# The up projection of a ConvFFN in seven block products, and its down projection after a detour through device memory

## The chip, the cores and the metric

The kernel runs on one core of one Trainium2 chip, as one program. The metric is the device time of one execution in microseconds. Three runs of the kernel before took 1481.65, 1480.47 and 1481.75 us (median 1481.65).

The engines are named as the profile names them: PE (TensorE, matrix products; PEld its weight loads), DVE (VectorE), ACT (ScalarE), POOL (GpSimd) and SP (the queue that issues most DMAs).

## What is computed

One layer of a streaming encoder works on 1024 prompt rows and 64 sample rows of 1024 channels, in fp32. After an input projection, two convolution mixers and a merge, the ConvFFN follows, and a final norm:

```python
h = rms_norm(x, norm2_g)
f_gate, f_val = jnp.split(h @ w_up, 2, axis=-1)           # w_up: 1024 x 5632
f_gate, new_f = causal_dwconv(f_gate, st_f, dw_f)          # 3 taps along time
x = x + (jax.nn.silu(f_gate) * f_val) @ w_down             # w_down: 2816 x 1024
```

Outputs are the normed rows of both groups and the last rows that each convolution saw.

## The kernel before

Activations lie with channels on the 128 partitions and time along the free dimension, W = 1092 columns (two rows of history, 1024 prompt rows, two of history, 64 sample rows). 1024 channels are KD = 8 tiles, the 2816 channels of the ConvFFN are KF = 22 feature tiles. An fp32 product is made from three reduced ones: each operand is split into a high half (rounded to the matmul's type) and a low half (the rest), and `products` (line 396) issues weight-high x activation-high, weight-high x activation-low, and weight-low x activation-high into one PSUM accumulation.

A "unit" (line 424) is one tile of 128 output channels over all columns: three thirds of 364 columns (362 in the first), for each third 8 k tiles of 3 matmuls, 72 matmuls in all. Units use the three PSUM banks of X and the three of Y in turn; S is a third, smaller area. For each unit SP loads 512 KB of weights (`load`, line 275), ACT makes the high half (`split_hi`, line 699), DVE the low half (`split_lo`, line 959), both two units ahead; semaphores count each step.

The ConvFFN stage starts at unit N_F. A loop over eleven groups (`ffn_units`, line 635) takes two feature tiles per turn: gate unit, value unit, gate unit, value unit, and between the first and the second the down projection of the group before (`down`, line 622): 8 output tiles x 3 thirds x 2 k tiles x 3 matmuls, added to the residual by DVE (`add_down`, line 1267). The residual `stream` and the running squares of the rows are kept on chip. The first gate unit starts third by third as the last unit of w_o is added up (lines 885 and 1214 to 1222). The reciprocal root of the mean square is not applied to h but to the products: column sums of squares on PE (`rms_columns`, line 601), `moments` on DVE (line 1132), a power on POOL (line 384), a diagonal matrix on DVE (line 1136), a row broadcast by PE (`rms_row`), and copies by ACT into rb2 (lines 913 and 914).

Per feature tile DVE multiplies the gate by rb2, puts in the two history columns, saves the last two, and applies three taps (lines 1229 to 1247); ACT takes silu (line 901); DVE multiplies by rb2 and by the value unit (lines 1251 and 1256); ACT and DVE split the result in halves (lines 905 and 957), which are the k tiles of the down projection. The last group is done in cuts of 386, 384 and 322 columns (lines 1324 to 1351), together with the transposes and the final norm of the output rows.

The order of the work on each engine is written out by hand; nothing is planned by a compiler.

Of the kernel before, what the change touches and what calls it, by code (L numbers as in the profile page):

```python
# [14 lines left out]
def streaming_encoder(nc: bass.Bass, ins, outs):  # L15
# [46 lines left out]
    G = KF // 2  # L62
# [6 lines left out]
    X_F1, Y_F1 = X_F0 + 2, Y_F0 + 2  # L69
    X_DL = X_F1 + 6 * (G - 1)  # L70
# [12 lines left out]
    Q_F = KB + 2 * KA  # L83
# [35 lines left out]
    q_hi, _ = place("q_hi", [P, KA, W], F32R)  # L119
# [3 lines left out]
    w_raw, _ = place("w_raw", [P, 2, KD * P], F32)  # L123
    w_hi, _ = place("w_hi", [P, 2, KD * P], F32R)
    w_lo, _ = place("w_lo", [P, 2, KD * P], F32R)
    t0, _ = place("t0", [P, W], F32)
    t1, _ = place("t1", [P, W], F32)
    xr, _ = place("xr", [P, 3 * D], F32)
# [4 lines left out]
    state_rows, _ = place("state_rows", [P, 4, P], F32)  # L133
# [7 lines left out]
    wd_raw = mid[:, 0:2 * D]  # L141
    wd_hi, _ = place("wd_hi", [P, 2, D], F32R, mid_at + 4 * 2 * D)
    wd_lo, _ = place("wd_lo", [P, 2, D], F32R, mid_at + 4 * 4 * D)
    rb2 = mid[:, 6 * D:6 * D + W]
    gf_row = mid[:, 6 * D + SW:7 * D + SW]
    assert 7 * D + SW <= KD * W
    out_rows, _ = place("out_rows", [P, NT, D], F32, h_at)
# [15 lines left out]
    sl, ac = xr[:, 0:W], xr[:, W:2 * W]  # L163
# [3 lines left out]
    half = stats[:, 5 * NT:6 * NT]  # L167
    ST_B = 2 * HA * KA
# [10 lines left out]
    with ExitStack() as ctx:  # L179
        X = ctx.enter_context(nc.psum_tensor("X", [P, CHUNKS, 512], F32))  # L180
        Y = ctx.enter_context(nc.psum_tensor("Y", [P, CHUNKS, 512], F32))
# [34 lines left out]
        value_part, ac_part, qhi_part, qlo_part = sem("value_part"), sem("ac_part"), sem("qhi_part"), sem("qlo_part")  # L216
        last_added = sem("last_added")

# [19 lines left out]
        F_STEPS = 6  # L238
# [28 lines left out]
        def _(sp):  # L267
# [51 lines left out]
            with sp.Fori(0, G) as i:  # L319
                load(w_up_cols, 2 * P * i, N_F, 4, i)  # L320
                load(w_up_cols, DF + 2 * P * i, N_F + 1, 4, i)
                load(w_up_cols, 2 * P * i + P, N_F + 2, 4, i)
                load(w_up_cols, DF + 2 * P * i + P, N_F + 3, 4, i)
                sp.wait_ge(hlo_done, KD)

                sp.dma_start(wd_raw.rearrange("p (k c) -> p k c", k=2),
                             w_down_rows[bass.ds(i, 1), :, :, :].rearrange("g p k c -> p (g k) c")
                             ).then_inc(wd_in, 16)
            sp.dma_start(gf_row, ins["final_g"].rearrange("(a d) -> a d", a=1).to_broadcast([P, D])).then_inc(gf_in, 16)

            n_out = 0
            sp.wait_ge(s_out, S_STATE + 1)
            for s, group in enumerate(("p", "s")):
                sp.dma_start(outs[f"new_conv_a_{group}"].rearrange("l b r (c p) -> (l b r c) p", p=P),
                             state_rows[0:HA * KA, s, :]).then_inc(stored, 16)
                sp.dma_start(outs[f"new_conv_b_{group}"].rearrange("l b r (c p) -> (l b r c) p", p=P),
                             state_rows[s * H * KB:(s + 1) * H * KB, 2, :]).then_inc(stored, 16)
            sp.wait_ge(s_out, S_FST + 1)
            for s, group in enumerate(("p", "s")):
                sp.dma_start(outs[f"new_ffn_conv_{group}"].rearrange("l b r (c p) -> (l b r c) p", p=P),  # L340
                             state_rows[s * H * KF:(s + 1) * H * KF, 3, :]).then_inc(stored, 16)
# [53 lines left out]
        def _(pe):  # L395
# [191 lines left out]
            unit(N_WO + 1, 2, i, y_out, Y_WO + i, KD, h_hi, h_lo, part=wo_part)  # L587

# [8 lines left out]

            def ffn_in(c):
                return lambda k: pe.wait_ge(hlo_done, KD + KD * c + k + 1)
# [6 lines left out]
            def rms_row(part):  # L606
                def run():
                    if part == 0:
                        pe.wait_ge(stat_step, KD + 2)
                    pe.wait_ge(s_out, S_R2 + part)  # L610
                    row_of(diag, part)()
                return run

            unit(N_F, 0, 0, x_out, X_F0, KD, h_hi, h_lo, (None, None, rms_columns), before=ffn_in)
            unit(N_F + 1, 0, 0, y_out, Y_F0, KD, h_hi, h_lo, (rms_row(0), rms_row(1)))
            unit(N_F + 2, 0, 0, x_out, X_F0 + 1, KD, h_hi, h_lo)
            unit(N_F + 3, 0, 0, y_out, Y_F0 + 1, KD, h_hi, h_lo)
# [3 lines left out]

            def down(group, x_use, y_use):

                pe.wait_ge(wdlo_done, group + 1)
                pe.wait_ge(qlo_done, KB + 2 * KA + 2 * group + 2)
                for m in range(KD):
                    b, free, uses = ((Y, y_out, y_use), (X, x_out, x_use))[m % 2]
                    pe.wait_ge(free, uses + m // 2)
                    for c in range(CHUNKS):
                        for k in range(2):  # L630
# [751 lines left out]
```

## Time and profile before

| | us |
|---|---|
| median of three runs | 1481.65 |
| span of the profiled execution, first to last instruction | 1479.4 |
| PE busy / PEld busy | 1456.1 / 1448.6 |
| DVE busy / ACT busy / POOL busy | 781.2 / 308.7 / 26.4 |
| ConvFFN: its first matmul starts | 665.41 |
| last group's tail: its first matmul starts | 1436.69 |

The profiled execution's own time is not listed apart from its span; the runs lie 1.1 to 2.4 us above the span. Busy time counts an engine's recorded instructions; overlapping ones count once. The end of a matmul is modelled, so recorded durations (330 ns for 364 columns) are longer than the step from one start to the next. "Idle before" is the time that an engine had nothing running ahead of an instruction, and the arrow names what ended it.

### The profile page before, as it was taken

To read this page: it belongs to the slowest core of one execution; us is meant where nothing else is said; L and a number is where in the kernel's file an instruction comes from. 1 tells how busy PE (TensorE), PEld (TensorE's weight loads), DVE (VectorE), ACT (ScalarE), POOL (GpSimd) and SP (SyncE) were. 2 spreads that over 40 slices of the span, in tenths; PEclk is the share of its full clock that TensorE was granted. 3 is DMA by queue.
4 is the path that set the end of the run, shared out by engine and by line. 5 is a ranking of instruction groups with operands and counts; after the bars stand their busy time and mean duration, and the time that the engine had idled before them with its cause. 6 is when DMAs were issued, how large, how long until landed. Compare 5 with 4: busy or idle time off the path is not lost.

```text
span 1479.4 us, 20930 instructions
## 1 busy us (share of the span) xinstructions
PE 1456.1 (98%) x8774; PEld 1448.6 (98%) x8774; DVE 781.2 (53%) x744; ACT 308.7 (21%) x329; POOL 26.4 (2%) x57
## 2 busy tenths in 40 slices
PE   6999999999999999999999999999999999999997
PEld 6999999999999999999999999999999999999997
DVE  5575888755642225346635363545454535354545
ACT  5321111111252214134111111111111111101012
POOL 3000000000000000000000000000000000000001
PEclk9999999999999999999999999999999999999999
DMA  5111111111022222112202020201010101010103
GB/s 188 53 43 43 43 43 43 41 45 43 29 72 71 71 71 64 43 43 72 72 15 71 14 71 14 71 26 59 28 57 28 57 28 57 28 57 29 61 2 121
DMA packets 107898, 77.18 MB, mean 52 GB/s; under 512 B 2469, under 2 KB 101527, under 8 KB 107863
## 3 DMA queue, kind: packets, MB, share of 16 engines
q1 hardware_dynamic: 106631, 72.22, 15.6%
q10 hardware_dynamic: 1232, 4.46, 0.9%
q8 instruction: 26, 0.43, 0.1%
q14 instruction: 9, 0.07, 0.0%
HBM read 72.04 MB, written 4.63 MB: 52 GB/s over the span
## 4 chain that ended last, share of the span: by engine, by line
PE 98%; DVE 1%; DMA 0%; POOL 0%; ACT 0%; issue 0%; DVEq 0%; SPq 0%
PE X L400 48%; PE Y L400 47%; PE S L562 1%; DMA xr<-in_x_prompt 0%; PE S L510 0%; PE Y L455 0%; DVE out_rows L1336 0%; PE S L668 0%; PE S L528 0%; PE Y L668 0%; POOL stats L377 0%; PE S L455 0%; DVE h_lo L957 0%; ACT h_hi L717 0%; DVE res L1345 0%
## 5 line engine op out<-in xcount | busy, mean ns | idle before, releaser
L400 PE MATMUL X<-h_hi,w_hi 128*128 128x364 f32 (+1 forms) x1056 | 347.7, 329 | 2.6 <-issue 2.4
L400 PE MATMUL X<-h_lo,w_hi 128*128 128x364 f32 (+1 forms) x1056 | 348.3, 330 | 0.0
L400 PE MATMUL Y<-h_lo,w_hi 128*128 128x364 f32 (+3 forms) x1056 | 347.6, 329 | 0.0
L400 PE MATMUL Y<-h_hi,w_hi 128*128 128x364 f32 (+3 forms) x1056 | 347.3, 329 | 0.0
L400 PE MATMUL X<-h_hi,w_lo 128*128 128x364 f32 (+1 forms) x1056 | 346.9, 329 | 0.0
L400 PE MATMUL Y<-h_hi,w_lo 128*128 128x364 f32 (+3 forms) x1056 | 346.3, 328 | 0.0
L957 DVE TENSOR_TENSOR w_lo<-w_raw,w_hi 128x1024 fp32r<-128x1024 f32 (+1 forms) x104 | 118.7, 1142 | 415.5 <-ACT w_hi L704 415.5
L704 ACT ACTIVATE w_hi<-w_raw 128x1024 fp32r<-128x1024 f32 (+1 forms) x104 | 103.2, 993 | 798.7 <-PE Y L400 485.9
L400 PEld LDWEIGHTS X<-h_hi,w_hi 128*128 128x128 f32 x1056 | 199.1, 189 | 3.4 <-issue 2.8
L400 PEld LDWEIGHTS Y<-h_hi,w_hi 128*128 128x128 f32 x1056 | 198.5, 188 | 0.6 <-issue 0.5
L400 PEld LDWEIGHTS X<-h_hi,w_lo 128*128 128x128 f32 x1056 | 199.0, 188 | 0.0
L400 PEld LDWEIGHTS X<-h_lo,w_hi 128*128 128x128 f32 x1056 | 199.0, 188 | 0.0
L400 PEld LDWEIGHTS Y<-h_lo,w_hi 128*128 128x128 f32 x1056 | 198.4, 188 | 0.5 <-issue 0.5
L400 PEld LDWEIGHTS Y<-h_hi,w_lo 128*128 128x128 f32 x1056 | 198.4, 188 | 0.0
L1010 DVE SCALAR_TENSOR_TENSOR res<-mid,cols,res 128x1118 f32<-128x1118 f32 (+1 forms) x120 | 165.7, 1381 | 18.0 <-DVE res L1010 17.8
L400 PE MATMUL X<-q_hi,wd_hi 128*128 128x364 f32 (+4 forms) x276 | 91.1, 330 | 0.0
L400 PE MATMUL X<-q_lo,wd_hi 128*128 128x364 f32 (+4 forms) x276 | 91.0, 330 | 0.0
L400 PE MATMUL X<-q_hi,wd_lo 128*128 128x364 f32 (+4 forms) x276 | 90.6, 328 | 0.0
L400 PE MATMUL Y<-q_lo,wd_hi 128*128 128x364 f32 (+4 forms) x252 | 83.1, 330 | 0.0
L400 PE MATMUL Y<-q_hi,wd_hi 128*128 128x364 f32 (+4 forms) x252 | 83.0, 329 | 0.0
L400 PE MATMUL Y<-q_hi,wd_lo 128*128 128x364 f32 (+4 forms) x252 | 82.7, 328 | 0.0
L1272 DVE TENSOR_TENSOR res<-X,res 128x1092 f32<-128x1092 f32 x40 | 51.8, 1294 | 39.4 <-PE X L400 39.3
(166 smaller groups left out, 1380.4 us busy)
## 6 DMA issues: line engine op xcount, KB each, us to landing
w_raw<-in_w_up SPq DMA_DIRECT2D x44, 512.0 KB, 3.7
w_raw<-in_w_in SPq DMA_DIRECT2D x36, 512.0 KB, 3.7
mid<-in_w_down SPq DMA_DIRECT2D x11, 1024.0 KB, 5.9
xr<-in_x_prompt SPq DMA_DIRECT2D x8, 512.0 KB, 3.8
xr<-in_x_prompt ACTq DMA_DIRECT2D x8, 512.0 KB, 4.3
w_raw<-in_w_o SPq DMA_DIRECT2D x8, 512.0 KB, 3.4
out_y_prompt<-out_rows SPq DMA_DIRECT2D x8, 512.0 KB
w_raw<-in_w_b_out SPq DMA_DIRECT2D x8, 256.0 KB, 2.6
```

The source lines that it names most:

```text
L400: done = pe.matmul(dst, w, act[:, k, cols[0]:cols[1]], start=(first and p == 0), stop=(last and p == 2))
L562: last = pe.transpose(S[:, k // 4, (k % 4) * P:(k % 4) * P + rows], xr[0:rows, s * D + k * P:s * D + (k + 1) * P], ident[0:rows, 0:rows])
L704: act.activation(w_hi[:, s, 0:k_tiles * P], w_raw[:, s, 0:k_tiles * P], ACT.Copy).then_inc(whi_done, 1)
L957: dve.tensor_tensor(out, full, hi.bitcast(F32), ALU.subtract).then_inc(done, 1)
L1010: dve.scalar_tensor_tensor(dst, mid[:, bass.ds(U_AT + c * UW + k, CVW)], col("dw_a", k * KA + c), dst, ALU.mult, ALU.add).then_inc(tap_don ...
L1272: dve.tensor_tensor(x, bank(bk), x, ALU.add).then_inc(out, 1)
```

## The change

**w_up in seven block products.** For one feature tile f, the gate tile and the value tile are computed together. The 8 k tiles are halved into even and odd ones, the 1092 columns into two halves of HB = 546, and the 256 output channels into value and gate. This is a product of 2x2 blocks, which is now made from seven block products (Strassen's scheme) in place of eight. The seven activation factors (-A11, S_1, S_2, S_4, S_3, A12, A22; the S are sums and differences of quarter blocks of the activation) are made once, with high and low halves. For each feature tile the seven weight factors are made from four loaded blocks b11, b12, b21, b22 of 256 KB by four sums of 512 columns on DVE (`up_sum`), seven high halves on ACT (`up_hi`) and seven low halves on DVE (`up_lo`), into a ring of seven places. Each product is 2 cuts (274 and 272 columns) x 4 k tiles x 3 matmuls; three of the seven accumulate on an earlier one in PSUM. ACT copies four partial results to SBUF (`copy_partial`), DVE combines them into gate and value (`combine`, OUT12, OUT22, OUT11, OUT21).

**The gated product goes to device memory.** The gated tile is stored to a new array `kept` (559 KB per feature tile), waits behind the next tile's weight loads on SP, and is loaded again after the up projection.

**w_down afterwards.** It runs in blocks of 7, 7, 6 and 2 feature tiles. In the first three, a unit is one output tile over three thirds with 7 (or 6) k tiles; the last 2 tiles are done in the old tail. Matmul widths stay as before.

The three small transposes of the convolution state are now issued before the last w_o unit. The code, cut to its core:

```diff
+            def up_load(k_half, n_half, g):
+                c = DF + P * g if n_half == 0 else P * g
+                sp.dma_start(raw_block(k_half, n_half).rearrange("p (k c) -> p k c", k=HK),
+                             w_up_cols[:, k_half, :, c:c + P]).then_inc(up_in[k_half][n_half], 16)
+            def next_loads(g):
+                sp.wait_ge(u_sum, SUMS * g - 3)
+                sp.wait_ge(u_lo, PRODUCTS * g - 6)
+                up_load(0, 0, g)
...
+            def keep_product(f):
+                sp.wait_ge(u_val, f + 1)
+                sp.dma_start(kept[f, :, :], prod_t).then_inc(p_out, 16)
...
+            for g in range(2, KF):
+                next_loads(g)
+                keep_product(g - 2)
...
+            down_load(1)
+            keep_product(LAST_F - 1)
+            for k in range(D_TILES[0]):
+                sp.wait_ge(u_prod, PRODUCTS * LAST_F + k // 2 + 1)
+                product_load(0, k)
...
+            def up_product(i, v, first, slot_lo=None):
+                a_hi, a_lo = slot(i, 0), slot(i, 1)
+                for c, (c0, c1) in enumerate(HALF_CUTS):
+                    at_ = 1024 * v + V_AT
+                    for k in range(HK):
...
+                        for p, (part, act) in enumerate(((0, a_hi), (0, a_lo), (1, a_hi))):
+                            last = pe.matmul(XY_flat[:, at_ + c0:at_ + c1], ring(i, part)[:, w], act[:, k, c0:c1],
...
+            def up(f, parity):
+                v = pairs_of(parity)
+                pe.wait_ge(u_lo, PRODUCTS * f + 1)
+                pe.wait_ge(u_copy, 4 * f)
+                up_product(0, v[0], True)
+                pe.wait_ge(u_lo, PRODUCTS * f + 2)
+                pe.wait_ge(u_comb, 4 * f - 4 + OUT11)
+                up_product(1, v[1], True)
+                pe.wait_ge(u_lo, PRODUCTS * f + 3)
+                pe.wait_ge(u_copy, 4 * f + CX1)
+                up_product(2, v[2], False)
+                pe.wait_ge(u_lo, PRODUCTS * f + 4)
+                pe.wait_ge(u_copy, 4 * f + CY1)
+                up_product(3, v[3], False)
+                pe.wait_ge(u_lo, PRODUCTS * f + 5)
+                pe.wait_ge(u_copy, 4 * f + CX2)
+                up_product(4, v[4], False)
...
```

ScalarE's and VectorE's order for one feature tile (g is the next tile, whose weights are made beside the products of f):

```diff
+            def up(f, parity):
+                v, g = pairs_of(parity), f + 1
+                copy_partial(f, CX1, v)
+                up_hi(g, 0)
+                copy_partial(f, CY1, v)
+                up_hi(g, 1)
+                copy_partial(f, CX2, v)
+                up_hi(g, 2)
+                act.wait_ge(u_prod, PRODUCTS * f + 4)
+                up_hi(g, 3)
+                copy_partial(f, CX3, v)
+                up_hi(g, 4)
+                act.wait_ge(u_prod, PRODUCTS * f + 6)
+                up_hi(g, 5)
+                up_silu(f)
+                act.wait_ge(u_prod, PRODUCTS * f + 7)
+                up_hi(g, 6)
...
+            def up(f, parity):
+                v, g = pairs_of(parity), f + 1
+                up_sum(g, 1)
+                up_lo(g, 0)
+                up_lo(g, 1)
+                up_sum(g, 2)
+                up_lo(g, 2)
+                combine(f, OUT12, v)
+                up_lo(g, 3)
+                up_sum(g, 3)
+                combine(f, OUT22, v)
+                gate_conv(f)
+                up_lo(g, 4)
+                combine(f, OUT11, v)
+                up_lo(g, 5)
+                up_sum(g, 4)
+                combine(f, OUT21, v)
+                up_lo(g, 6)
+                gated_value(f)
```

Here gate_conv is the multiply by rb2, the small copies and the three taps, and gated_value the two multiplies, as before. At the start of the stage VectorE's order behind the last w_o unit, and ScalarE's around the first silu:

```diff
+            s_sum_of(i, S_1)
+            s_sum_of(i, S_2)
+            slot_lo(S_1, i)
+            s_sum_of(i, S_4)
+            slot_lo(S_2, i)
+            slot_lo(S_4, i)
+            up_lo(0, 3)
             add_squares(i, 1)
+            dve.wait_ge(stat_step, KD + 1)
+            up_sum(0, 3)
+            s_sum_of(0, S_3)
...
+            slot_lo(S_3, 3)
+            up_lo(0, 4)
             moments(S_MS, D, RMS_EPS)
...
             dve.wait_ge(s_out, S_R2 + 2)
+            dve.memset(act_t[:, 0:H], 0.0)
+            gate_conv(0)
+            up_sum(1, 1)
+            up_lo(1, 0)
...
+            act.wait_ge(stored, 64)
+            up_hi(0, 6)
             copy_row(rb2, S_R2, 0, 1.0, W)
             copy_row(rb2, S_R2, 1, 1.0, W)
...
+            up_hi(1, 4)
+            up_silu(0)
+            up_hi(1, 5)
+            act.wait_ge(u_prod, PRODUCTS)
+            up_hi(1, 6)
```

At the last feature tile ScalarE and VectorE also split the first block of reloaded tiles (down_hi, down_lo: 1092 columns each):

```diff
+            copy_partial(LAST_F, CX1, v)
+            split_hi(N_F, k_tiles=D_TILES[0])
+            copy_partial(LAST_F, CY1, v)
+            down_hi(0)
+            copy_partial(LAST_F, CX2, v)
+            down_hi(1)
+            down_hi(2)
+            copy_partial(LAST_F, CX3, v)
...
+            gate_conv(LAST_F)
+            down_lo(2)
+            combine(LAST_F, OUT11, v)
+            split_lo(N_F + 1, k_tiles=D_TILES[0])
+            down_lo(3)
+            combine(LAST_F, OUT21, v)
+            for t in range(4, D_TILES[0]):
+                down_lo(t)
+            gated_value(LAST_F)
...
+            for b in range(D_FULL):
+                n = N_F + KD * b
+                for u in range(2):
+                    tiles = (lambda k: pe.wait_ge(d_lo, D_FIRST[b] + k + 1)) if u == 0 else None
+                    if b == 0:
+                        down_unit(n + u, b, 0, u_comb, 4 * LAST_F + (OUT11, OUT21)[u], tiles)
...
```

## Rows read from the trace of the kernel before

**Rows 1.** The page's busy line of the engines and its chain by engine.

```profile
PE 1456.1 (98%) x8774; PEld 1448.6 (98%) x8774; DVE 781.2 (53%) x744; ACT 308.7 (21%) x329; POOL 26.4 (2%) x57
...
PE 98%; DVE 1%; DMA 0%; POOL 0%; ACT 0%; issue 0%; DVEq 0%; SPq 0%
```

**Rows 2.** Busy time by stretch: us, each engine's busy time (instructions), clock, DMA share, GB/s.

```profile
18.00:22.40 4.40, 3.77 (x12) 3.73 (x13) 3.96 (x4) 2.29 (x5) 3.59 (x4) 1.00 0.33 117
...
200.00:260.00 60.00, 60.00 (x363) 60.00 (x362) 52.53 (x48) 9.49 (x9) 0.00 (x0) 1.00 0.16 46
...
836.00:1420.00 584.00, 584.00 (x3510) 584.00 (x3509) 283.70 (x267) 87.61 (x75) 0.00 (x0) 1.00 0.14 43
```

**Rows 3.** Timeline of TensorE, first and last 322-column matmul of a run: start us, us.

```profile
1458.45 0.31 PE L400 MATMUL X<-q_lo,wd_hi 128*128 128x322 f32 x1
...
1460.81 0.31 PE L400 MATMUL Y<-q_hi,wd_lo 128*128 128x322 f32 x1
```

**Rows 4.** Instruction groups of TensorE by shape: count | busy us, mean ns | idle.

```profile
L400 PEld LDWEIGHTS X<-h_hi,w_hi 128*128 128x128 f32 x1056 | 199.1, 189 | 3.4 <-issue 2.8 <-DVE h_lo L957 0.5
...
L562 PE MATMUL S<-ident,xr 128*128 128x128 f32 x64 | 8.3, 272 | 0.0
...
L528 PE MATMUL S<-ones,res 128*128 128x1 f32 x18 | 2.1, 245 | 0.0
```

**Rows 5.** Instruction groups of VectorE by shape.

```profile
L1246 DVE SCALAR_TENSOR_TENSOR t<-t,cols,t 128x1090 f32<-128x1090 f32 x44 | 59.4, 1351 | 2.6
...
L1251 DVE TENSOR_TENSOR xr<-xr,mid 128x1092 f32<-128x1092 f32 x22 | 28.3, 1287 | 1.2 <-ACT xr L901 1.2
...
L1221 DVE SCALAR_TENSOR_TENSOR h_lo<-res,cols,h_hi 128x364 fp32r<-128x364 f32 x24 | 12.4, 588 | 0.0
...
L957 DVE TENSOR_TENSOR w_lo<-w_raw,w_hi 128x512 fp32r<-128x512 f32 x16 | 11.1, 691 | 100.1 <-ACT w_hi L704 100.1
```

**Rows 6.** Timeline, one gate chain in the ConvFFN loop, ScalarE and VectorE.

```profile
849.44 1.06 ACT L704 ACTIVATE w_hi<-w_raw 128x1024 fp32r<-128x1024 f32 x1 [4.41 <-PE X L400]
...
850.53 1.23 DVE L957 TENSOR_TENSOR w_lo<-w_raw,w_hi 128x1024 fp32r<-128x1024 f32 x1 [4.17 <-ACT w_hi L704]
...
851.68 1.29 DVE L1231 TENSOR_TENSOR t<-X,mid 128x1092 f32<-128x1092 f32 x1
...
854.51 2.83 DVE L1246 SCALAR_TENSOR_TENSOR t<-t,cols,t 128x1090 f32<-128x1090 f32 x2
```

**Rows 7.** Instruction groups of ScalarE by shape.

```profile
L901 ACT ACTIVATE xr<-t 128x1092 f32<-128x1092 f32 x22 | 24.6, 1120 | 157.9 <-DVE t L1246 157.9
...
L704 ACT ACTIVATE w_hi<-w_raw 128x512 fp32r<-128x512 f32 x16 | 10.1, 631 | 127.8 <-PE X L400 68.3 <-PE Y L400 59.5
...
L799 ACT ACTIVATE res<-S 128x1024 f32<-128x1024 f32 x2 | 2.1, 1028 | 7.2 <-PE S L510 7.2
...
L901 ACT ACT_TABLE_LOAD x1 | 1.3, 1283 | 0.0
```

**Rows 8.** DMA issues: count, KB each, median us to landing.

```profile
w_raw<-in_w_up SPq DMA_DIRECT2D x44, 512.0 KB, 3.7
...
w_raw<-in_w_b_out SPq DMA_DIRECT2D x8, 256.0 KB, 2.6
```

**Rows 9.** Timeline at the turn from w_o to the ConvFFN.

```profile
665.17 0.38 PE L594 MATMUL S<-ident,state 128*120 128x128 f32 x2
...
665.41 0.41 PE L400 MATMUL X<-h_hi,w_hi 128*128 128x362 f32 x1
...
681.70 1.36 DVE L1138 TENSOR_TENSOR xr<-ident,stats 128x1152 f32<-128x1152 f32 x1 [1.92 <-POOL stats L384]
```

**Rows 10.** Timeline of TensorE at the start of the run.

```profile
18.63 0.64 PE L400 MATMUL X<-h_hi,w_hi 128*128 128x364 f32 x1 [2.42 <-issue]
19.07 0.51 PE L400 MATMUL X<-h_lo,w_hi 128*128 128x364 f32 x1
...
22.10 0.51 PE L400 MATMUL X<-h_hi,w_lo 128*128 128x364 f32 x1
```

More of the change, by code:

```diff
@@ L82, in streaming_encoder @@
     SKIP = (NT + 1) // 2
-    Q_F = KB + 2 * KA
+    HB = W // 2
+    HK = KD // 2
+    HALF_CUTS = [(0, 274), (274, HB)]
+    V_AT = 512 - HALF_CUTS[0][1]
+    assert HB * 2 == W and (HB - 274) % 2 == 0 and HB - 274 <= 512
+    PRODUCTS = 7
+    SUMS = 4
+    S_MINUS_A11, S_1, S_2, S_4, S_3, S_A12, S_A22 = range(PRODUCTS)
+    CX1, CY1, CX2, CX3 = range(1, 5)
+    OUT12, OUT22, OUT11, OUT21 = range(1, 5)
+    D_TILES = [7, 7, 6, 2]
+    D_FIRST = [sum(D_TILES[:b]) for b in range(len(D_TILES))]
+    D_FULL = len(D_TILES) - 1
+    assert sum(D_TILES) == KF and max(D_TILES) <= KD and D_TILES[-1] == 2
     PACKS = [
@@ L606, in rms_row @@
             def rms_row(part):
[L607 to L616, printed above, removed]
@@ L619, in down_weights @@
             def down_weights(k, m):
                 return wd_hi[:, k, m * P:(m + 1) * P], wd_lo[:, k, m * P:(m + 1) * P]
[L622 to L630, printed above, removed]
-                            last = products(b[:, c, third(c)[0] - c * CW:CW], down_weights(k, m), (q_hi, q_lo),
-                                            third(c), k, k == 0, k == 1)
-                    last.then_inc(down_done, 1)
@@ new lines, in copy_partial @@
+            def copy_partial(f, which, v):
+                act.wait_ge(u_prod, PRODUCTS * f + {CX1: 1, CY1: 2, CX2: 3, CX3: 5}[which])
+                if which == CX3:
+                    act.wait_ge(u_comb, 4 * f + OUT12)
+                elif not (isinstance(f, int) and f == 0):
+                    act.wait_ge(u_comb, 4 * f - 4 + {CX1: OUT11, CY1: OUT22, CX2: OUT21}[which])
+                dst = {CX1: x1_t, CY1: y1_t, CX2: x23_t, CX3: x23_t}[which]
+                act.activation(dst[:, :], pair(v[{CX1: 0, CY1: 1, CX2: 2, CX3: 4}[which]]),
+                               ACT.Copy).then_inc(u_copy, 1)
@@ L879, in _ @@
+            for i in range(KD // 2 - 1):
                 for u in range(2):
@@ new lines, in s3_hi, with plain_hi @@
+            def s3_hi(j):
+                act.wait_ge(s_sum, 3 * HK + j + 1)
+                slot_hi(S_3, j)
+            def plain_hi(i, half, j):
+                act.activation(slot(i, 0)[:, j, :], stream[:, 2 * j + 1, half * HB:(half + 1) * HB], ACT.Copy,
+                               scale=col("norm2_g", 2 * j + 1)).then_inc(s_hi, 1)
+            minus_a11_again(0)
+            minus_a11_again(1)
+            copy_partial(0, CY1, v)
+            minus_a11_again(2)
+            minus_a11_again(3)
@@ L1206, in _ @@
+            for i in range(KD // 2 - 1):
                 for u in range(2):
@@ new lines, in _ @@
+            up_lo(0, 4)
+            moments(S_MS, D, RMS_EPS)
+            plain_lo(S_A12, 0, 0)
+            plain_lo(S_A12, 0, 1)
+            diagonals(stat_step, NT + 2, diag2[:, :])
+            plain_lo(S_A12, 0, 2)
+            plain_lo(S_A12, 0, 3)
+            up_lo(0, 5)
+            up_sum(0, 4)
+            v = pairs_of(0)
+            combine(0, OUT12, v)
+            for j in range(HK):
+                plain_lo(S_A22, 1, j)
+            up_lo(0, 6)
+            combine(0, OUT22, v)
```

644 lines of the change are left out of this document (430 added, 214 removed).

## Prediction, made before the changed kernel was run

> **What bounds the kernel now.** I read the page's busy line and its chain first, then busy time by stage, then the timelines at the edges of the stage that changes. TensorE is 98% busy and holds 98% of the chain that ends last [rows 1]. VectorE and ScalarE have 53% and 21%. Busy TensorE need not mean a full one, so I count starts: the stretch from 836 to 1420 us, all inside the ConvFFN loop, holds 3510 matmuls in 584.0 us, 166.4 ns each, with clock 1.00 [rows 2]. The stretch from 200 to 260 us, where VectorE is 88% busy, has 363 in 60 us, 165.3 ns: a busy VectorE does not slow the matmuls. So every matmul slot that disappears is worth 166 ns, as long as no wait comes in its place; today there is none: TensorE is busy for 584.00 of those 584.00 us.
>
> **What a matmul of the new width costs.** This decides most. The old ones have 362 or 364 columns (mean 363.3), the new ones 274 or 272 (mean 273), each with its own weight load. The narrowest in the trace have 322: 17 starts from 1458.45 to 1460.81 us, 16 steps of 147.5 ns [rows 3]. 147.5/322 and 166.4/363.3 are both 0.458 ns per column, with nothing left over per instruction, so 273 columns give 125.0 ns. From below the nearest rows are the transposes of 128 columns, each with its own load: 64 in eight bursts of 8.3/8 = 1.04 us, whose last matmul lasts 0.27, so (1.04-0.27)/7 = 110 ns; matmuls of one column with a load each take 2.1/18 = 117 ns [rows 4]. A load therefore hides beneath a matmul of 125 ns, though narrowly. Bounds 110 and 147.5 ns; I take 125, because two widths lie on one line through zero.
>
> The weight loads are 98% of the span too, 189 ns each [rows 1, 4]: longer than the 147.5 ns between starts in rows 3, so their recorded times overlap and do not add up. The Trainium skill ("Perfetto Trace Analysis", Identifying the Most-Contended Engine) holds the busy share of weight loads for a good measure of how full TensorE is. By that rule more loads could not be cheaper, which is the first rival below.
>
> **Products of w_up.** Removed: 44 units of 72 matmuls, 3168 x 166.4 ns = 527.1 us. Added: 22 feature tiles of 7 products, each 4 k tiles x 2 cuts x 3 terms = 24 matmuls; 3696 x 125.0 = 462.0 us, 21.0 us per tile, 3.0 per product. Difference -65.1 us. w_down keeps its 1584 matmuls at the old widths, and the sums over columns and rows stay: 0.
>
> **Does the steady state keep TensorE fed?** VectorE per tile: 4 weight sums and 7 low halves of 512 columns at 0.69 us, 4 combinations of 546 columns at 0.73 (between 0.69 at 512 and 1.29 at 1092) [rows 5], the gate chain from multiply to last tap 5.7 (851.68 to 857.34) [rows 6], two products of 1.29: 7.6+2.9+5.7+2.6 = 18.8 of 21.0 us. ScalarE: 7x0.63 + 4x0.65 + 1.12 = 8.1 [rows 7]. New w_up tiles have a period's slack, since a ring place is refilled when its product is done and is used one tile later. The tight ring is this: end of the fifth product, ScalarE's copy of it 0.65, OUT22 0.73, gate chain 5.7, a low half 0.69, OUT11 0.73, with about 0.2 of hand-over: 8.7 us; OUT11 frees the bank for the next tile's second product, and four products (12.0) later the fifth ends again. 20.7 against 21.0: just covered, at no cost. If the chain grows past 9.0 us, each further us costs 1 us per tile. The store of the gated tile (559 KB) and four loads of 256 KB fit easily: 256 KB land in 2.6 us and 512 in 3.7, so 2.2 us per further 512 KB, and 559 KB are 3.9 us alone and 2.4 behind others [rows 8]. SP issues the store behind the next tile's loads, some 7.6 us into the next tile, when VectorE has its product; it lands well ahead of the next OUT11 at 23 us.
>
> **Start of the stage.** Before, TensorE went from w_o into w_up with a step of 0.24 us [rows 9]. Now the sums of activation halves come first. Those of the first three tile pairs lie under w_o, whose two units last 24 us against some 13 us of VectorE and 8 of ScalarE per pair: 0. For the last pair I lay out the queues from the end of w_o (time 0), an instruction starting 0.08 us before its predecessor's recorded end unless it waits (850.53+1.23 against 851.68 [rows 6]); a slot sum of 546 columns is 0.78, between 0.59 at 364 and 1.35 at 1090 [rows 5].
> (a) VectorE: the last residual and ScalarE's source behind it, 1.4; three sums and three low halves, 4.3; a weight half, 6.4; the last squares, which wait for ScalarE, 8.4; a weight sum, 9.0; four S_3 sums and four low halves, 15.0; another weight half, 15.7. Product five needs that; TensorE gets there at 4x3.0 plus 1.3 of column sums and 0.2 of waiting before product three, 13.5. Waits: 0.2+2.2.
> (b) The row of reciprocal roots needs VectorE's moments, POOL's power (VectorE waited 1.92 us for it before [rows 9]) and the diagonals: 0.4 late. Product six waits 0.2 for its weights; the row's second part 1.5 for ScalarE's copy of the first (1.03 [rows 7]), which stands behind high halves. 2.1.
> (c) That copy is whole at 26.1; gate_conv(0) starts then and holds VectorE to 31.9. The weight sum and low half of tile 1 are queued behind it, so TensorE waits from 28.9 to 33.3: 4.4.
> (d) The second product of tile 1 waits 0.6 for OUT11(0); the third for ScalarE's copy of the first, queued behind the first silu with its table load of 1.28 [rows 7] and two high halves that wait for VectorE: 4.2.
> ScalarE's new wait for four small state stores comes some 20 us after their issue: 0. Sum 13.7 us.
>
> **End of the stage.** The tile kept last but one is stored at 7.6 us into tile 21, and seven product loads follow on SP. The first lands at 7.6+3.9+2.4 = 13.9; its high half stands on ScalarE ahead of the copy that product five waits for: 13.9+1.1+0.65 = 15.7 against 12.0, 3.7. The first w_down unit waits for OUT11, behind that chain and a 1092-column low half: 4.2; its k tiles 3 to 6 then wait for low halves at 1.2 us each, against 0.5 of matmul: 3.4. Sum 11.3. Later w_down units last 63 x 166 ns = 10.5 us and cover their 3.7 us of VectorE, 2.1 of ScalarE and 1 MB of loads.
>
> **Sum.** The page's span is 1479.4; the three runs are 1480.47 to 1481.75, so 1.1 to 2.4 us lie around it, and I set its own time at the median, 1481.65. 1481.65 - 65.1 + 13.7 + 11.3 = 1441.6, say 1442. Bounds: the 25 us of edge waits could be 12 (transfers earlier, queues overlapping better) or 35. The matmul at 110 ns would leave the VectorE ring as bound, 8.7 + 4x24x0.110 = 19.3 us a tile, 22x1.7 less, 1404 us; at 147.5 see next.
>
> **Rivals.**
> A, the load sets the pace: matmul steps stay at the 147.5 ns of rows 3. 3696 x 147.5 = 545.2, +18 instead of -65; the edge waits shrink to some 20: 1520 us, **slower**. It ends on that side from 136 ns per matmul on ((527.1-25)/3696). For it: loads recorded at 189 ns, 117 ns with one column. Against: no fixed remainder at 322 and 363 columns.
> B, VectorE becomes the bound: 18.8 of 21.0 us in strict order, with the ring 0.3 us from its limit. With 1.2 us beyond that in it for hand-overs: 20 tiles x 1.2 = 24, 1466 us. For it: rows 5 and 6 were taken at half that load; against: a hand-over of 0.03 us, from 849.44+1.06 to 850.53 [rows 6].
> C, restarts at half pace. Behind 2.42 us of idle time the first twelve matmuls of 364 columns step by 303 ns (ten steps from 19.07 to 22.10 [rows 10]), though the clock column says 1.00 from 18 to 22.4 us [rows 2]. Five new waits are longer than 2 us; 12 x (303-166) ns = 1.6 us each gives 8 us more: 1450 us. For it: those rows; against: they are the first large matmuls of the run. The Trainium skill ("TensorE: Matmul & The Clock Gate", Loop structure matters more than you think) lets TensorE go cold in long waits between bursts; no row here shows a wait of 2 to 4 us in mid-run.
>
> **How the numbers follow.** Forecast 0.67, A 0.08, B 0.13, C 0.12. The forecast's own range, edge waits 12 to 35 and step 124 to 127 ns, is 1425 to 1459. C lies in it; to reach most of B the top goes to 1466. Left out: A and the far part of B and of the forecast, about 2 in 10. Slower by over 0.2% (3 us, what a measurement of this kernel tells from no change): A, 0.08. Same: 0.02, a step near 136. Faster: 0.90.
>
> **What would show it.** Right: matmul steps of 125 ns, seven products in 21 us, TensorE without gaps from the third tile to the last, VectorE near 85% there, gaps of 4 us at the first silu and at the turn to w_down. A shows as steps near 148 with unbroken weight loads; B as a gap before the second product of every tile, ended by VectorE; C as doubled steps behind a gap. The prediction is wrong if steps exceed 130 ns or the gaps sum to over 40 us.

## The result, and the profile after

Measured: 1446.86 us (median of 4 runs, 1444.76 to 1447.66) against 1481.06 us for the kernel before (4 runs beside them, 1480.34 to 1481.75). The ratio is 0.9766, 95% interval 0.9754 to 0.9778. Forecast were 1442.0 us, 1425 to 1466, with 0.90 on faster. The profiled run took 1446.4 us, its span is 1444.3; from span to span the change gives 1479.4 - 1444.3 = 35.1 us, where the forecast had 65.1 - 13.7 - 11.3 = 40.1.

The page after, busy line and chain, to be held against [rows 1]:

```profile
PE 1404.6 (97%) x9302; PEld 1393.9 (97%) x9302; DVE 892.8 (62%) x1006; ACT 421.4 (29%) x555; POOL 26.8 (2%) x57
...
PE 92%; DVE 4%; ACT 1%; issue 1%; DMA 1%; POOL 0%; SPq 0%; DVEq 0%; ACTq 0%
```

TensorE runs 528 matmuls more than before in 51.5 us less of busy time: they are narrower. Its share of the chain fell from 98% to 92%, VectorE's rose from 1% to 4%: waits that did not exist before. The weight loads' share fell by one point while their count rose by 528.

Busy time by stretch, after (columns as in [rows 2]): the start of the stage, the middle of w_up, and three short pieces right behind waits.

```profile
665.00:720.00 55.00, 44.72 (x310) 42.13 (x309) 44.96 (x65) 29.78 (x47) 2.28 (x1) 0.94 0.17 49
...
720.00:1120.00 400.00, 400.00 (x3156) 400.00 (x3154) 327.73 (x451) 145.10 (x226) 0.00 (x0) 1.00 0.24 76
...
699.20:702.60 3.40, 3.40 (x15) 3.40 (x16) 2.60 (x5) 1.15 (x2) 0.00 (x0) 0.53 0.30 80
...
710.50:713.00 2.50, 2.50 (x13) 2.50 (x13) 2.47 (x3) 0.56 (x2) 0.00 (x0) 0.50 0.20 59
1146.90:1149.80 2.90, 2.90 (x14) 2.90 (x14) 2.11 (x3) 1.58 (x2) 0.00 (x0) 0.50 1.03 423
```

In the middle TensorE never stops: 400.00 / 3156 = 126.7 ns for a matmul, 168 of them 21.3 us for a tile. VectorE is 82% busy there and no wait of TensorE's is put down to it. At the edges it is different, and not by the idle time alone: in the last three lines TensorE counts as fully busy, yet starts a matmul only every 190 to 230 ns, and the granted clock is 0.50 (1.2 of 2.4 GHz) or just above. Such steps are called half-pace steps below.

TensorE's timeline at tile 1 (start us, us; in brackets the idle time before and what ended it), and from tile 21 into w_down:

```profile
699.18 4.81 PE L747 MATMUL XY<-sa,w_hi 128*128 128x274 f32 x24 [3.72 <-DVE w_hi L1243]
703.83 3.19 PE L747 MATMUL XY<-sa,w_lo 128*128 128x274 f32 x24
710.08 4.62 PE L747 MATMUL XY<-sa,ring_x 128*128 128x274 f32 x24 [3.06 <-ACT t L1092]
...
1146.50 4.79 PE L747 MATMUL XY<-sb,w_lo 128*128 128x274 f32 x24 [2.48 <-ACT t L1092]
1151.13 6.27 PE L747 MATMUL XY<-sb,ring_x 128*128 128x274 f32 x48
1159.81 0.63 PE L530 MATMUL XY<-down,w_hi 128*128 128x362 f32 x2 [2.40 <-issue]
```

The four long waits of the forecast stand where it put them, each shorter than forecast (4.4, 4.2, 3.7, 4.2). A product between waits lasts 3.2 us on this view; the ones right behind a wait 4.6 to 4.8, and that was only a rival. The idle time in the whole ConvFFN stretch is 16.4 us; before it was none.

Why the third product of tile 1 waits is seen on ScalarE, same kernel:

```profile
704.53 1.28 ACT L1097 ACT_TABLE_LOAD   x1
705.83 1.12 ACT L1097 ACTIVATE u_t<-u_t 128x1092 f32<-128x1092 f32 x1
...
708.88 0.63 ACT L1083 ACTIVATE ring_x<-sum_a 128x512 fp32r<-128x512 f32 x1 [1.42 <-DVE sum_a L1538]
709.42 0.61 ACT L1092 ACTIVATE t<-XY 128x546 f32<-128x546 f32 x1
```

The copy at 709.42 (line 1092) reads a product that was done at 704.0; it stands behind the table load, the silu and a high half that itself waits for VectorE.

### The profile page after: what moved, and what is told of

It is laid out like the page before. It is cut to its first block, busy times and chain, and to the rows that moved or that the text cites. A ratio compares the mean times of both kernels' runs of the same rounds, so it can differ in the third digit from the quotient of the medians.

```text
span 1444.3 us, 23045 instructions
## 1 busy us (share of the span) xinstructions
PE 1404.6 (97%) x9302; PEld 1393.9 (97%) x9302; DVE 892.8 (62%) x1006; ACT 421.4 (29%) x555; POOL 26.8 (2%) x57
## 4 chain that ended last, share of the span: by engine, by line
PE 92%; DVE 4%; ACT 1%; issue 1%; DMA 1%; POOL 0%; SPq 0%; DVEq 0%; ACTq 0%
PE XY L530 61%; PE XY L747 29%; PE S L692 1%; DMA xr<-in_x_prompt 0%; DVE out_rows L1732 0%; PE XY L585 0%; DVE down L1591 0%; DMA down_f<-kept 0%; DVE sb L1519 0%; DVE u_t L1577 0%; DVE w_lo L1243 0%; ACT t L1092 0%; PE S L845 0%; DVE u_t L1564 0%; PE S L640 0%
## 5 line engine op out<-in xcount | busy, mean ns | idle before, releaser
L530 PE MATMUL XY<-h_hi,w_hi 128*128 128x364 f32 (+1 forms) x1056 | 348.6, 330 | 2.6 <-issue 2.4
L530 PE MATMUL XY<-h_lo,w_hi 128*128 128x364 f32 (+1 forms) x1056 | 348.3, 330 | 0.0
L530 PE MATMUL XY<-h_hi,w_lo 128*128 128x364 f32 (+1 forms) x1056 | 347.0, 329 | 0.0
L530 PE MATMUL XY<-down,w_hi 128*128 128x364 f32 (+1 forms) x960 | 238.4, 329 | 3.6 <-issue 2.4
L530 PEld LDWEIGHTS XY<-h_hi,w_hi 128*128 128x128 f32 x1056 | 199.0, 188 | 3.8 <-issue 3.0
L530 PEld LDWEIGHTS XY<-h_lo,w_hi 128*128 128x128 f32 x1056 | 199.0, 188 | 0.2 <-issue 0.2
L530 PEld LDWEIGHTS XY<-h_hi,w_lo 128*128 128x128 f32 x1056 | 199.0, 188 | 0.0
L530 PEld LDWEIGHTS XY<-down,w_hi 128*128 128x128 f32 x960 | 169.9, 189 | 4.9 <-issue 2.6
L530 PE MATMUL XY<-down,w_lo 128*128 128x364 f32 (+1 forms) x480 | 157.7, 329 | 0.0
L747 PE MATMUL XY<-sa,w_hi 128*128 128x272 f32 (+1 forms) x1056 | 142.6, 291 | 3.7 <-DVE w_hi L1243 3.7
```

Source lines behind the costliest of these rows:

```text
L530: done = pe.matmul(dst, w, act[:, k, cols[0]:cols[1]], start=(first and p == 0), stop=(last and p == 2))
L747: last = pe.matmul(XY_flat[:, at_ + c0:at_ + c1], ring(i, part)[:, w], act[:, k, c0:c1], start=(first and k == 0 and p == 0), stop=(k == H ...
```

## The experiments

"The changed kernel" is the 1446.86 us one. Each run was timed beside the kernel before, whose medians lie between 1480.98 and 1481.36 us.

**Is the wait at the first silu one of order?** One copy moved on ScalarE:

```diff
             up_hi(1, 4)
+            copy_partial(1, CX1, pairs_of(1))
             up_silu(0)
```

> ScalarE copies the first product of tile 1 before the silu of tile 0 instead of after it; nothing else moves. Theory (the forecast's d: tile 1's third product waits 3.06 us for that copy because it stands behind the table load and the silu): the wait goes, and the 12 matmuls that then stepped at 228 ns instead of 127 go with it, so 3.1 + 1.3 = 4.4 us less than the changed kernel, 1442.5 us. Rival: the low half of the third block on VectorE, which is also behind gate_conv(0), is almost as late as the copy; then the wait stays at 2 us or more and the time falls by 1 us or less.

Measured 1442.75 us (5 runs, 1442.31 to 1444.38), 4.1 less than the changed kernel; against the kernel before 0.9745 (0.9731 to 0.9758). The time fits the theory, the trace only half:

```profile
706.78 3.19 PE L747 MATMUL XY<-sa,ring_x 128*128 128x274 f32 x24
711.04 3.28 PE L747 MATMUL XY<-sa,w_hi 128*128 128x274 f32 x24 [1.06 <-ACT t L1092]
715.05 1.15 PE L747 MATMUL XY<-sb,w_lo 128*128 128x274 f32 x7 [0.73 <-ACT t L1092]
...
1144.35 2.88 PE L747 MATMUL XY<-sb,w_lo 128*128 128x274 f32 x21 [2.78 <-ACT t L1092]
```

The third product starts at once, but the next two copies, still behind the silu, make waits of 1.06 and 0.73 us. Tile 1 gets 2.4 us shorter (first product to the next tile's first: 27.56 to 25.18). Another 1.2 us comes from a place that was not touched: behind the 2.78 us of idle time before product five of tile 21 no half-pace steps follow this time (21 matmuls in 2.88 us).

**Are both waits of tile 1 of order?** On VectorE, and with a second early copy on ScalarE:

```diff
-            dve.wait_ge(s_out, S_R2 + 2)
-            dve.memset(act_t[:, 0:H], 0.0)
-            gate_conv(0)
+            dve.wait_ge(u_lo, PRODUCTS)
             up_sum(1, 1)
             up_lo(1, 0)
...
             up_sum(1, 3)
+            dve.wait_ge(s_out, S_R2 + 2)
+            dve.memset(act_t[:, 0:H], 0.0)
+            gate_conv(0)
             up_lo(1, 4)
```

> VectorE prepares tile 1's first four weight blocks before gate_conv(0) instead of behind it, and ScalarE makes tile 1's first two copies before the silu of tile 0. Theory (the forecast's c and d are waits of order alone, not of throughput): tile 1's first product (3.72 us idle, then 16 steps of 227 ns) and its third (3.06 us, then 12 steps of 228 ns) both start at once: 3.7 + 1.7 + 3.1 + 1.3 = 9.8 us less than the changed kernel, 1437 us. Rival: VectorE is full in the first two tiles, so that the 5.1 us of gate_conv(0) put behind the blocks only shift the wait to a later product of tile 1 or 2: 4 us or less gained.

Measured 1443.22 us (1438.71 to 1443.84), 3.6 less: the rival's figure. The traces put it a little higher: the first three tiles get 4.6 us shorter (82.8 to 78.2, from the first product of w_up to the first of tile 3), and 1.1 us are lost again at the turn to w_down, which was not touched, with half-pace steps behind a wait of 2.80 us and among the first of w_down. Even 4.6 is less than half of the 9.8 that the theory gives. TensorE in this kernel, and busy time by stretch:

```profile
715.21 3.27 PE L747 MATMUL XY<-sb,ring_x 128*128 128x274 f32 x24 [1.31 <-DVE u_t L1560]
718.32 3.20 PE L747 MATMUL XY<-sa,w_hi 128*128 128x274 f32 x24
723.93 4.32 PE L747 MATMUL XY<-sa,w_lo 128*128 128x274 f32 x21 [2.41 <-DVE u_t L1567]
...
1142.45 4.80 PE L747 MATMUL XY<-sb,w_lo 128*128 128x274 f32 x24 [2.80 <-ACT t L1092]
```

```profile
684.00:732.00 48.00, 42.40 (x306) 40.23 (x305) 44.24 (x63) 21.37 (x34) 0.03 (x1) 0.96 0.25 75
```

VectorE in this kernel:

```profile
714.35 0.72 DVE L1560 TENSOR_TENSOR u_t<-XY,t 128x546 f32<-128x546 f32 x1
...
716.94 1.30 DVE L1574 TENSOR_TENSOR u_t<-u_t 128x1092 f32<-128x1092 f32 x1
...
719.80 2.84 DVE L1587 SCALAR_TENSOR_TENSOR u_t<-u_t,cols 128x1090 f32<-128x1090 f32 x2 [0.15 <-DVE u_t L1584]
...
723.16 0.72 DVE L1567 TENSOR_TENSOR u_t<-XY,t 128x546 f32<-128x546 f32 x1
```

Both waits at the start of tile 1 are gone. New ones come at its seventh product and at tile 2's second; the latter waits for OUT11 (line 1567), which stands behind tile 1's gate chain from 716.94. VectorE is busy for 44.2 of the 48 us from 684 to 732, against 39.6 in the changed kernel. So the waits that the forecast priced singly are for the most part one delay of VectorE's, and moving one item hands it on.

**The turn to w_down.** On SyncE, ScalarE and VectorE:

```diff
-            keep_product(LAST_F - 1)
             for k in range(D_TILES[0]):
+                if k == 4:
+                    keep_product(LAST_F - 1)
...
-            down_hi(0)
             copy_partial(LAST_F, CX2, v)
...
             combine(LAST_F, OUT22, v)
+            down_lo(3)
+            combine(LAST_F, OUT11, v)
...
+            split_lo(N_F + 1, k_tiles=D_TILES[0])
             gate_conv(LAST_F)
-            down_lo(2)
...
```

> At the turn to w_down: SyncE issues the first reloads before the store of tile 20, ScalarE makes the copy CX2 of tile 21 before the high halves of the reloaded products and the silu of tile 21 after them, VectorE makes the low halves and the sums OUT of tile 21 before its convolution. Theory (all end waits are waits of order): product five of tile 21 (2.48 us idle and 13 steps of 228 ns), the first w_down unit (2.40 us idle and some 9 steps of 302 ns for 167) and the three waits for low halves (0.35 + 0.44 + 0.45) go: 2.5 + 1.3 + 2.4 + 1.3 + 1.2 = 8.7 us less than the changed kernel, 1438 us. Rival: the transfers of the turn set it, since the first reloaded tile lands only at 1144.7: then the waits for low halves grow, and 3 us or less are gained.

Measured 1437.60 us (1435.58 to 1438.53), 9.3 less, 0.9706 (0.9692 to 0.9719) of the kernel before. TensorE, from the last two products on:

```profile
1146.88 6.25 PE L748 MATMUL XY<-sb,ring_x 128*128 128x274 f32 x48
1152.97 0.48 PE L531 MATMUL XY<-down,w_hi 128*128 128x362 f32 x2
...
1156.37 0.59 PE L531 MATMUL XY<-down,w_hi 128*128 128x362 f32 x2 [0.28 <-DVE down L1591]
```

Of five waits, 6.1 us together, one of 0.28 is left, and w_down's first matmul follows the last product without a gap. The theory holds, size included. The same without SyncE's part:

> As the kernel with the turn to w_down reordered, but SyncE issues the reloads behind the store of tile 20 as the changed kernel does. Theory (the order on ScalarE and VectorE is the whole cause): 1437.6 us within 1. Rival (the reloads' landing at 1144.7 us, behind that store, sets the low halves): some 2 to 4 us more, 1440 to 1442, with waits for low halves of the first k tiles back in the first w_down unit.

Measured 1439.66 us (1436.06 to 1440.01), 2.1 above the full edit. In the traces the ConvFFN stretch differs by 2.7 us: 1.4 are half-pace steps at tile 1 (25 against 11), where both kernels are alike and which must count as chance, and 1.3 lie at the turn, where a wait of 0.63 us before w_down and one of 0.44 for a low half are back. The order on ScalarE and VectorE is most of the gain; the reloads' landing is worth some 1.3 us, not 2 to 4.

**Does standing still cause the slow steps?** Matmuls of 512 columns whose sums are never read, put into three of the long waits:

```diff
+            def filler(count):
+                for _ in range(count):
+                    pe.matmul(S[:, 1, :], slot(S_A22, 0)[:, 0, 0:P], slot(S_A22, 0)[:, 0, 0:512], start=True, stop=True)
...
+            filler(14)
+            up(1, 1)
```

> 14, 11 and 9 matmuls of 512 columns whose sums nobody reads are put into three of the long waits (before tile 1's first product, before its third, before product five of tile 21); the waits themselves stay. Rival C of the forecast (TensorE restarts at half pace because it stood still): the steps after these three waits stay at about 127 ns instead of 227 for 16, 12 and 13 steps, so 1.6 + 1.2 + 1.3 = 4.1 us less than the changed kernel, 1442.8 us. Rival to it: the slow steps have another cause in those moments (operands still arriving, the other engines' traffic): steps still at 227 ns and the time unchanged, or longer where the added matmuls outlast the wait.

Measured 1444.24 us (1444.09 to 1445.75), 2.6 less. Timeline of TensorE, and busy time by stretch:

```profile
675.90 4.72 PE L747 MATMUL XY<-sa,w_hi 128*128 128x274 f32 x24
...
694.52 3.35 PE L754 MATMUL S<-sb 128*128 128x512 f32 x14
698.32 3.31 PE L747 MATMUL XY<-sa,w_hi 128*128 128x274 f32 x24 [0.45 <-DVE w_hi L1255]
702.02 3.27 PE L747 MATMUL XY<-sa,w_lo 128*128 128x274 f32 x24 [0.40 <-DVE u_t L1569]
705.14 2.68 PE L754 MATMUL S<-sb 128*128 128x512 f32 x11
709.40 3.28 PE L747 MATMUL XY<-sa,ring_x 128*128 128x274 f32 x24 [1.58 <-ACT t L1104]
```

```profile
677.30:680.60 3.30, 3.30 (x15) 3.00 (x14) 2.91 (x6) 2.63 (x6) 0.00 (x0) 0.50 0.00 0
...
699.20:702.60 3.40, 3.00 (x24) 2.81 (x23) 2.70 (x5) 1.15 (x2) 0.00 (x0) 1.00 0.29 77
710.50:713.00 2.50, 2.50 (x22) 2.50 (x21) 2.47 (x4) 0.36 (x1) 0.00 (x0) 1.00 0.09 33
1146.90:1149.80 2.90, 2.90 (x25) 2.90 (x25) 1.40 (x3) 1.74 (x3) 0.00 (x0) 1.00 1.03 422
```

The clock is 1.00 in the very stretches that had 0.50, with nearly the same traffic beside it in the first and the last line (77 and 80, 422 and 423 GB/s), and the products last 3.3 us. So the slow steps in these three places come from TensorE's own standing still, and not from operands or traffic. The gain is 2.6 and not 4.1, since the first restart's 1.6 us come to nothing: the third product of tile 1 waits for ScalarE's copy, and it starts 44.8 and 44.9 us after the first product of w_up in the two kernels. In the traces tile 1 gets 1.2 us shorter and tile 21 1.3; the time alone would not show it, since the slowest of these runs is slower than the fastest of the changed kernel. The Trainium skill ("TensorE: Matmul & The Clock Gate", Loop structure matters more than you think) says that a long wait for a DMA between matmuls makes TensorE go cold; these lines agree, for waits on VectorE and ScalarE.

A wait is not needed for half pace, though. In this trace the product at 675.90 (the fourth of tile 0) steps at half pace from 677.3 on at a clock of 0.50, with no idle time right ahead of it; what TensorE did before were the products of tile 0 and, from 673.97 to 676, eighteen matmuls of one column. Two of the other traces (the narrow products and the longer ring below) show the same, the rest do not. It cost nothing here, because the next product would have waited 1.5 us anyway.

**What sets the step?**

```diff
-                for c, (c0, c1) in enumerate(HALF_CUTS):
+                for c, (c0, c1) in enumerate(HALF_CUTS if slot_lo else ((0, 200), (274, 514))):
```

> From tile 1 on the two halves of each block product have 200 and 240 columns instead of 274 and 272: the products leave out columns 200 to 273 and 514 to 545, so the up-projection is computed in part only and the time is not that of the reference's work. All instructions stay. What is asked is the step from one matmul to the next. Theory (the step follows its columns along one line, 0.44 ns a column and 6.7 ns for each instruction, through the steps of 273, 322 and 363 columns): 95 ns at 200 columns and 112 ns at 240. Rival A in its milder form (the weight load sets a floor under the step, which the 273 columns already feel): no step below some 110 ns at 200 columns, and 115 or more at 240. The tile is then bound by VectorE's ring: 20.8 us less what four products shrink by (4 x 0.55), 18.6 us, or by VectorE's own busy time, 17.5 us, if the ring is no bound.

One run, 1410.3 us; the kernel leaves out part of the up projection. Timeline of TensorE, a group of it by shape, and busy time by stretch:

```profile
743.71 1.53 PE L747 MATMUL XY<-sa,w_hi 128*128 128x240 f32 x12
745.96 2.96 PE L747 MATMUL XY<-sa,w_lo 128*128 128x200 f32 x24 [0.71 <-DVE u_t L1557]
748.75 2.85 PE L747 MATMUL XY<-sa,ring_x 128*128 128x200 f32 x24
751.44 0.82 PE L747 MATMUL XY<-sa,w_hi 128*128 128x200 f32 x6
```

```profile
L747 PE MATMUL XY<-sa,w_hi 128*128 128x240 f32 x444 | 56.7, 277 | 0.0
```

```profile
740.00:1100.00 360.00, 351.14 (x3091) 347.58 (x3091) 319.56 (x444) 137.66 (x221) 0.00 (x0) 1.00 0.26 80
```

Twelve matmuls of 240 columns last 1.53 us with the last one's 0.277 in it: (1.53 - 0.277)/11 = 114 ns a step. A whole product takes 751.44 - 748.75 = 2.69 us, so the twelve of 200 columns step by (2.69 - 12 x 0.114)/12 = 110 ns. The line's 112 and 95 fail at the narrow end: a floor of 110 ns lies there, the same as the transposes' 110 in [rows 4]. That the weight load sets this floor, as the milder rival A says, is not shown: no run left the loads out.

The filler above adds a wider row: 14 matmuls of 512 columns last 3.35 us, the last one 0.39, so (3.35 - 0.39) / 13 = 228 ns a step. A line from there to 126.7 at 273 columns falls by 0.42 ns a column and leaves 11 ns for each instruction. It gives 147.5 ns at 322 columns, 165 at 363 and 113 at 240, each within 2 ns of what was measured; at 200 it gives 96, against 110. So each instruction does have a remainder, and the floor adds some 14 ns at 200 columns but hardly 1 at 240.

The tile takes 360 / 3091 x 168 = 19.6 us here and waits for OUT11 (line 1557) before its second product. By the forecast's ring it is 20.8 - 4 x (3.04 - 2.69) = 19.4; VectorE alone, 17.5 us, would have let it go faster.

**Is the ring as tight as forecast?**

```diff
                 dve.wait_ge(u_comb, 4 * f + OUT22)
+                if not isinstance(f, int):
+                    dve.tensor_scalar(gate_t[:, :], gate_t[:, :], 1.0, None, ALU.mult).then_inc(u_more, 1)
+                    dve.wait_ge(u_more, f)
```

> One more pass of VectorE over the gate values (a multiplication by 1.0, 1092 columns, about 0.8 us by the tensor-scalar row of the convolution) stands ahead of gate_conv in 20 of the 22 tiles. Theory (the ring from product five over OUT22, the convolution and OUT11 to the next tile's second product is nearly as long as the tile: 0.5 us of slack at 21.31 us): the ring becomes the longer one by 0.8 + 0.1 - 0.5 = 0.4 us a tile, 20 x 0.4 = 8 us more than the changed kernel, 1455 us, with a wait of about 0.4 us before the second product of every tile. Rival (VectorE only has to keep up in throughput, and it has 3.8 us free in each tile): no wait, no change.

Measured 1455.81 us (4 runs, 1451.87 to 1456.09), 9.0 more; 1451.87 is the profiled one.

```profile
720.00:1100.00 380.00, 377.97 (x2945) 374.01 (x2944) 319.48 (x441) 134.90 (x210) 0.00 (x0) 1.00 0.24 74
```

380.00 / 2945 x 168 = 21.68 us a tile, 0.38 more than the changed kernel's 21.3, as the theory said; VectorE is busy for 319.48 of 380, so it is the ring and not its load. The idle time shown is only 2.03 us in 17.5 tiles, 0.12 each: a matmul is recorded with 0.29 us and stepped after 0.127, so the first 0.16 us of any wait hide under the last matmul's record, and the first step behind a wait takes 0.23 us, 0.10 more. In the profiled run the products last 6.1 us longer altogether, about 7.5 from tiles 2 to 21 less 1.3 in tile 1, where its second wait is shorter (1.91 us) and brings no half-pace steps; the 4 us more of the other three runs have no profile.

**Both edits, and more of them.**

> The edits of the start and of the end together. They lie 420 us apart, so their gains should add: the start alone gave 3.6 us, the end alone 9.3, so 1446.9 - 3.6 - 9.3 = 1434.0 us. If one of them had gained only by shifting the other's waits, the sum would stay 2 us or more short of it.

Measured 1431.69 us (1431.04 to 1433.07), 15.2 less than the changed kernel: the gains add, with 2.3 us over. In the traces the first three tiles get 4.7 us shorter, as with the start edit alone, and the turn 8.9, as with the end edit alone; 1.1 of the 2.3 are what the profiled run of the start edit alone had lost at the turn, and the rest lies within the spread of the runs.

For the delay of VectorE that is left, GpSimd makes the sums of tiles 1 and 2:

```diff
+            for g in (1, 2):
+                pool.wait_ge(u_lo, PRODUCTS * g)
...
+                pool.tensor_tensor(sum_a[:, :], b11, b12, ALU.add).then_inc(u_sum, 1)
```

> As the kernel with both edits, and GpSimd, idle there, makes the eight sums of weight blocks of tiles 1 and 2 in place of VectorE. Theory (with the start reordered, VectorE is short of time in the first three tiles, not badly ordered: it showed hardly any idle time from 684 to 732 us): 8 x 0.6 = 4.8 us of it freed, of which the waits left there (1.3, 2.4 and 1.3 us of slow steps) take up 3 to 5: 1429 to 1431 us. Rival (what is late there is a chain of waits, of which the sums are no part, or GpSimd's sums come later than VectorE's would): no gain, 1434 us or above.

Measured 1432.86 us (1432.51 to 1433.18), 1.2 more than both edits: no gain, as the rival says (its 1434 counts from the 1434.0 expected of both edits, not from the 1431.69 measured). GpSimd, VectorE and TensorE in this kernel:

```profile
708.33 2.27 POOL L521 TENSOR_TENSOR sum_a<-w_raw 128x512 f32<-128x512 f32 x1 [8.11 <-DVE ring_x L1266]
...
714.35 1.28 POOL L525 TENSOR_TENSOR t<-w_raw 128x512 f32<-128x512 f32 x1
```

```profile
708.17 1.29 DVE L1607 TENSOR_TENSOR u_t<-u_t 128x1092 f32<-128x1092 f32 x1
709.50 2.26 DVE L1610 TENSOR_TENSOR u_t<-u_t 128x1092 f32<-128x1092 f32 x1
...
715.09 1.08 DVE L1266 TENSOR_TENSOR ring_x<-sum_a,ring_x 128x512 fp32r<-128x512 f32 x1 [2.13 <-ACT ring_x L1097]
716.10 0.71 DVE L1575 TENSOR_TENSOR u_t<-XY,t 128x546 f32<-128x546 f32 x1
```

```profile
716.96 4.80 PE L761 MATMUL XY<-sb,ring_x 128*128 128x274 f32 x24 [1.97 <-DVE u_t L1575]
```

A sum that VectorE makes in 0.69 us takes GpSimd 1.28, and 2.27 where a VectorE instruction with two operands in SBUF runs beside it; VectorE then stands idle for 2.13 us, and OUT12 behind it ends a wait of TensorE's of 1.97 us, with 16 half-pace steps behind (24 matmuls in 4.80 us). Two VectorE instructions of one shape take 1.29 and 2.26 us: the second waits for the GpSimd sum to end (708.33 + 2.27 = 710.60, and 709.50 + 2.26 - 1.29 = 710.47). The Trainium skill ("SBUF — State Buffer", Who interferes with whom) says that a VectorE instruction with two inputs in SBUF contends with a GpSimd instruction that reads SBUF, and of the port pair that they share that whoever issues first has it for the whole instruction; these lines agree.

Instead, tile 1's own sums go ahead of its convolution:

```diff
+            combine(1, OUT12, v)
+            up_sum(2, 1)
...
+            combine(1, OUT22, v)
...
+            combine(1, OUT11, v)
...
+            gate_conv(1)
```

> The kernel with both edits, and tile 1's work on VectorE and ScalarE reordered too: the sums OUT12, OUT22 and OUT11 of tile 1 before its convolution, and the first two copies of tile 2 before the silu of tile 1. Theory (the waits left in tiles 1 and 2, 1.3 and 2.4 us with 1.3 us of slow steps, come from sums that stand behind other VectorE work, and VectorE, with 3.8 us free in each later tile, can make the delay up there): 3 to 5 us less than with both edits, 1427 to 1429 us. Rival (VectorE simply has more work in these tiles than TensorE, whatever the order): the same waits appear one tile later, 1431 to 1432 us.

Measured 1428.88 us (1428.50 to 1429.14), 2.8 less than both edits; 0.9646 (0.9633 to 0.966) of the kernel before and 18.0 us below the changed kernel. Of the waits in tiles 1 and 2 one remains:

```profile
729.92 3.31 PE L748 MATMUL XY<-sb,w_lo 128*128 128x274 f32 x24 [1.48 <-ACT t L1093]
```

No step of w_up runs at half pace in this trace, and tiles 3 to 20 last 21.31 us each as before. Order does help, then, where it lets the delay run into later tiles, in which VectorE has time to spare.

## Why the prediction was right, and where its terms were off

The sign, the mechanism and the range hold; the sum was 5.0 us too good, and its parts were off by more.

**The step** failed in size. "Two widths lie on one line through zero" gave 125.0 ns; it is 126.7, and 3696 of them take 468.3 us for 462.0, 6.3 more. The two widths lie 41 columns apart, and the 322-column steps are sixteen of one short piece at the run's end; that was too little to tell "nothing left over per instruction" from the 11 ns that the 512-column matmuls show. The lower bound, 110 ns from the transposes, proved to be a real floor.

**The steady state** held: no gap from the third tile to the last, VectorE at 82% for "near 85", the ring at 20.8 us for 20.7 (OUT11 ends 0.5 us before the next tile's second product). VectorE's load was summed too high, 18.8 us a tile (90% of 21.0, which "near 85" does not fit) for 17.5: recorded durations were added, though each next instruction starts some 0.08 us before the last one's recorded end, as the forecast itself read from [rows 6]. The ring was costed at nothing, rightly, and the added pass shows that a longer one would have cost 0.38 us a tile for some 0.9 of VectorE's time.

**The waits** were right in place and cause, too long in size: at the start 0.1 + 1.5 + 0.5 + 1.4 + 3.7 + 3.1 = 10.3 us idle for 13.7, at the end 2.5 + 2.4 + 1.2 = 6.1 for 11.3. The 3.4 us for four low halves are 2.8 by the forecast's own 4 x (1.2 - 0.5); three waits of 1.2 us together came. The forecast also let OUT11(0) hold the second product of tile 1 for 0.6; it did not. That they were waits of order was never said outright. At the turn one reordering takes nearly all of them away; at the start the first reordering takes 4.6 us off the first three tiles, and the one that reorders tile 1 too takes off 8.4 (82.8 to 74.4).

**Rival C** came true beside the forecast instead of in its place, and its chance of 0.12 was too low. The clock of 1.00 that the forecast saw beside the doubled steps of the run's start was no reading: in that trace the clock is on record from 24.04 us on. Behind the four waits of 2.4 us and more, 16, 11 and 13 steps of some 227 ns for 127 and 9 of 302 for 167 cost 40 x 0.10 + 9 x 0.135 = 5.2 us; the forecast's price was 8 for five.

The sum with the measured terms: 468.3 - 527.1 + 10.3 + 6.1 + 5.2 = -37.2; of each of the eleven waits 0.16 us do not show as idle, 1.8 together: -35.4, against -35.1 measured. The terms missed by +6.3, +5.2 and -8.6 + 1.8, so some of the nearness of 1442 to 1447 is luck.

**Rivals A and B** did not occur: no step near 147 ns at 273 columns, and no wait of TensorE's on VectorE from tile 2 to the end of w_up.

## What to carry to other kernels

When a stage gets faster than the engines that feed it at its edges, price the delay of the feeding engine over the first tiles as one sum, not each wait by itself: moving one instruction hands the delay on, and it is recovered only where later tiles have time to spare. A wait of TensorE's of some 2 to 4 us may cost another 1 to 2.5 us behind it, and need not: two traces of one kernel's unchanged part can differ by more than a microsecond for this alone, so hold the traces against each other piece by piece before a small gain is put down to an edit. Matmuls that nobody reads buy that back where the wait cannot be removed, unless another wait stands right behind. Do not read a step below the narrowest row off a line through two near widths: look for a far wider row, which shows the remainder, and for the row that shows the floor.

## What the runs showed of the hardware that was not expected

- Matmuls with a load each step by 228 ns at 512 columns, 126.7 at 273, 114 at 240 and 110 at 200: from 240 columns down, a narrower product saves next to nothing.
- Half pace does not follow every long wait. 2.48 us before product five of tile 21 brought 13 slow steps; 2.78 us at the same place, in the kernel with one moved copy, brought none. 1.97 us brought 16 in the kernel with GpSimd's sums; 1.91 us in the kernel with the longer ring brought none. And it can come without a wait, as in tile 0 of three traces. What tells these apart is open.
- A busy line of 100% can hide half pace: in 710.50 to 713.00 us TensorE is busy for 2.50 of 2.50 us with 13 matmuls, against 22 with the wait filled. The count of matmuls and the clock column show it, the busy time does not.
